# A two-block transformer step in fp32: selection in another order, a separate buffer at the seam between two product stages, and gate products among the stick-breaking items

## The reference, cut to what matters

```python
# PEER: 8 heads, 2 x 128 sub-keys, the top 16 of 16384 experts for each token and head
q = (t @ wq).reshape(128, 8, 2, 128)
s = einsum('tpcd,pckd->tpck', q, sub_keys)
s1, i1 = top_k(s[:, :, 0], 16);  s2, i2 = top_k(s[:, :, 1], 16)
top, pos = top_k(s1[..., :, None] + s2[..., None, :], 16)      # over 16 x 16 pairs
idx = i1 * 128 + i2 at pos;      g = softmax(top)
out = sum_k g_k * gelu(u[idx_k] . t) * v[idx_k]
...
# second block: projections of h, then
stick: z = q k / 8; w = sigmoid(z) * prod over later keys of sigmoid(-z), strictly causal; o_a = w v
soft:  an ordinary causal softmax over 64 + 32 (rotary) columns; q and k,v come from low-rank products
y_a = (o_a * silu(z_a)) @ w_branch_a;   y_b = (o_b * silu(z_b)) @ w_branch_b
x = x + gate * ((sigmoid(g_a) * y_a + sigmoid(g_b) * y_b) @ w_out);  out = rmsnorm(x)
```

## Time and profile before

| what | value |
|---|---|
| median of 3 runs | 2365.03 us (2364.62 to 2365.92) |
| the profiled execution's own time | 2369.11 us |
| its span, first to last instruction | 2367.3 us |
| mean granted TensorE clock in the span | 0.972 |

### The profile page before, as it was taken

How to read it: one execution, slowest core, us unless ns; L and a number is a source line. 1 busy time by engine, 2 the same in 40 slices (tenths; PEclk the granted TensorE clock), 3 DMA queues, 4 the chain that set the end, 5 groups by cost and what they waited for, 6 DMA issues and landing times. The chain is left out here.

```text
span 2367.3 us, 31784 instructions
## 1 busy us (share of the span) xinstructions
PE 2206.1 (93%) x12629; PEld 1966.4 (83%) x12629; DVE 1684.8 (71%) x2801; ACT 918.6 (39%) x1203; POOL 617.9 (26%) x354
## 2 busy tenths in 40 slices
PE   5999889988999998999999899999999896899997
PEld 2888777866799998999999899999999674576775
DVE  6555677873489999889876778788786656756543
ACT  4222234333233333566653233333333533576323
POOL 0000042322347667233333433333331000000000
PEclk8999999999999999999999999999999898899999
DMA  7567410012237777899999999999995222111222
GB/s 257 206 227 236 154 50 1 1 71 72 89 125 250 242 243 244 300 370 334 364 339 382 361 352 353 351 359 349 350 362 209 82 89 71 54 54 63 80 89 72
DMA packets 178100, 488.69 MB, mean 206 GB/s; under 512 B 13696, under 2 KB 80384, under 8 KB 166432
## 3 DMA queue, kind: packets, MB, share of 16 engines
q1 hardware_dynamic: 141088, 352.43, 43.6%
q0 software_dynamic: 36864, 134.23, 14.7%
HBM read 432.08 MB, written 52.43 MB: 205 GB/s over the span
## 5 line engine op out<-in xcount | busy, mean ns | idle before, releaser
L1087 PE MATMUL ps<-h_high,u_high 128*128 128x384 f32 (+1 forms) x1216 | 429.7, 353 | 21.7 <-POOL u_low L1305 11.9
L1089 PE MATMUL ps<-h_high,u_low 128*128 128x384 f32 (+1 forms) x1216 | 421.3, 346 | 0.0
L1088 PE MATMUL ps<-h_low,u_high 128*128 128x384 f32 (+1 forms) x1216 | 421.2, 346 | 0.0
L1087 PE MATMUL ps<-w_high,v_high 128*128 128x384 f32 x1024 | 343.6, 336 | 10.4 <-DVE w_low L1722 10.4
L1089 PE MATMUL ps<-w_high,v_low 128*128 128x384 f32 x1024 | 342.8, 335 | 0.0
L1088 PE MATMUL ps<-w_low,v_high 128*128 128x384 f32 x1024 | 342.8, 335 | 0.0
L1087 PEld LDWEIGHTS ps<-h_high,u_high 128*128 128x128 f32 x1216 | 231.5, 190 | 35.9 <-POOL u_low L1305 13.8
L1455 ACT ACTIVATE v_high<-v_raw 128x2048 fp32r<-128x2048 f32 x64 | 122.6, 1916 | 346.6 <-PE ps L1089 346.6
L1087 PE MATMUL ps<-h_high,w_high 128*128 128x512 f32 x560 | 226.7, 405 | 22.3 <-DVE w_low L346 7.5
L1089 PEld LDWEIGHTS ps<-h_high,u_low 128*128 128x128 f32 x1216 | 231.1, 190 | 8.1
L1088 PEld LDWEIGHTS ps<-h_low,u_high 128*128 128x128 f32 x1216 | 232.0, 191 | 7.1
(11 more groups left out here) (434 smaller groups left out, 4192.5 us busy)
## 6 DMA issues: line engine op xcount, KB each, us to landing
v_raw<-in_peer_v SPq DMA_DIRECT2D x64, 1024.0 KB
w_raw<-in_w SPq DMA_DIRECT2D x99, 512.0 KB, 3.5
u_first<-in_uT SPq DMA_DIRECT2D x32, 1024.0 KB
u_second<-in_uT SPq DMA_DIRECT2D x32, 1024.0 KB
xT<-in_late_w SPq DMA_DIRECT2D x56, 512.0 KB, 4.4
gelu_up<-gelu SPq DMA_DIRECT2D x128, 192.0 KB
gates<-gates_sb SPq DMA_DIRECT2D x12, 2048.0 KB, 12.6
weighted<-gelu_up SPq DMA_DIRECT2D x64, 384.0 KB
```

The source lines that it names most:

```text
L1087: pe.matmul(out, wh, mh, start=start, stop=False)
L1088: pe.matmul(out, wh, ml, start=False, stop=False)
L1089: return pe.matmul(out, wl, mh, start=False, stop=stop)
```

## The change

1. **Units.** They follow `UNIT_ORDER`: by head group over two token tiles (`SELF` and tile 0), then the other two tiles. The steps are 6, 7, 8, 9, 10, 12, 13, 15, 17, 20, 22, 24, 27, 29, 31, 34. The last unit of `SELF` is unit 5 at step 12 (`OWN_LAST`) where it was unit 3 at step 12.
2. **Picks.** 46 in steps 18 to 40, 66 in steps 41 to 68, 16 in steps 68 to 74. POOL issues the picks of a step after the low part of the next step.
3. **Batches** begin one tile later. `peer_v` rows begin at down step 1.
4. **The seam.** A buffer `gates_in` of its own takes the first gates, `gate_pair(0)` no longer waits for `u_raw`, `spill` runs one step earlier, and DVE and ACT prepare down step 1 before they turn to the dots and rows.
5. **Second block.** Two `uqm` tiles share a weight piece (4 pieces in place of 8). `ga` 0 and 1 and `sz` 0 to 2 (24 matmuls each) move to the first half, and slots are filled by the size of a product. `scores` of one item waits for its own bank alone, and DVE does `mask(n + 2)` right behind `finish(n)`.

```diff
-EARLY, MIDDLE = 40, 66
+FIRST_PICK, EARLY, MIDDLE = 18, 46, 66
+UNIT_ORDER = [(0, 0), (0, 1), (1, 0), (1, 1), (2, 0), (3, 0), (2, 1), (3, 1)] + [(c, t) for t in (2, 3) for c in range(4)]
+OWN_LAST = UNIT_ORDER.index((3, 0))
...
-    return OUT_G + 2 + 2 * u if u < 4 else OUT_G + 10 + 2 * (u - 4)
+    return OUT_G + (2, 3, 4, 5, 6, 8)[u] if u < 6 else OUT_G + 9 + 7 * (u - 6) // 3
...
-        return PICK_AT + (SPREAD_AT - PICK_AT) * n // EARLY
+        return FIRST_PICK + (SPREAD_AT - FIRST_PICK) * n // EARLY
...
-    return GROUPS - 7 + 7 * (n - EARLY - MIDDLE) // (PICKS - EARLY - MIDDLE)
+    return GROUPS - 8 + 7 * (n - EARLY - MIDDLE) // (PICKS - EARLY - MIDDLE)
...
-    return SPREAD_AT * EXPERT_TILES + m * SPREAD_G * EXPERT_TILES // BATCHES
+    return SPREAD_AT * EXPERT_TILES + 1 + m * (SPREAD_G * EXPERT_TILES - 1) // BATCHES
...
-    return n * (U_G - 3) // PICKS
+    return 1 + n * (U_G - 4) // PICKS
...
+        first_gates = sb("gates_in", [P, BLOCKS * 2 * GE * TB])
...
-                if g - 4 >= OUT_G + WQ_G:
-                    spill(g - 4)
+                if g - 3 >= OUT_G + WQ_G:
+                    spill(g - 3)
...
-            spill(GROUPS - 4)
+            gate_pair(0)
             load(0)
-
-            sp.wait_ge(u_split, OUT_PIECES + WQ_G + U_G - 1)
-            gate_pair(0)
             spill(GROUPS - 3)
             load(1)
             spill(GROUPS - 2)
-            sp.wait_ge(u_split, OUT_PIECES + WQ_G + U_G)
+            sp.wait_ge(u_split, OUT_PIECES + WQ_G + U_G - 1)
             gate_pair(1)
...
-                for n in picks_at[x + OUT_G]:
+                for n in picks_at[x + OUT_G - 1]:
...
+            high_v(1)
+            high_w(1)
             act.wait_ge(row_used, PICKS)
             act.activation(row_dot[:], row_dot[:], ACT.Gelu).then_inc(row_gelu, 1)
-            for g in range(1, U_G):
+            for g in range(2, U_G):
...
-            weigh(0)
-            low_v(0)
-            low_w(0)
+            for g in range(2):
+                weigh(g)
+                low_v(g)
+                low_w(g)
...
-    for h in range(NH):
-        piece("uq", h, [("uqm", h)])
-    for i in range(2):
-        piece("kn", i, [("kn", 4 * i + j) for j in range(4)])
+    for i in range(4):
+        piece("uq", i, [("uqm", 2 * i), ("uqm", 2 * i + 1)])
+    piece("kn", 0, [("kn", j) for j in range(4)])
+    piece("ga", 0, [("ga", 0)])
+    piece("sz", 0, [("sz", 0)])
+    piece("kn", 1, [("kn", 4 + j) for j in range(4)])
+    piece("ga", 1, [("ga", 1)])
     piece("kv", 0, [("kv", t) for t in range(4)])
-    for i in range(8):
+    for i in (1, 2):
+        piece("sz", i, [("sz", i)])
+    halfway = len(tiles)
+    for i in (2, 3):
         piece("ga", i, [("ga", i)])
...
                 for s in range(2):
+                    if p:
+                        pe.wait_ge(acted, 2 * p - 1 + s)
...
             def mask(n):
                 kind, h, i = items[n]
                 W = width(n)
-                dve.wait_ge(scored, 2 * (n // 2) + 2)
+                dve.wait_ge(scored, n + 1)
...
+            mask(0)
+            mask(1)
             for p in range(slots):
-                if p < PAIRS:
-                    mask(2 * p)
-                    mask(2 * p + 1)
                 for j in fill[p]:
                     if j in FIRST2:
                         low(TILES2[j][2] + 1)
                     evac(j)
+                for n in (2 * p, 2 * p + 1):
+                    if n < N:
+                        finish(n)
+                    if n + 2 < N:
+                        mask(n + 2)
                 if p >= 2 and (p - 2) % TT == TT - 1:
                     store((p - 2) // TT)
-                if p < PAIRS:
-                    finish(2 * p)
-                    finish(2 * p + 1)
```

More of the change, by code:

```diff
@@ L1257, in load @@
                 sp.dma_start(w[:, g % 2], gelu[g]).then_inc(w_in[g % 2], 16)
-            spill(GROUPS - 4)
+            written = 0
+            for g in range(GROUPS):
+                if g >= 2:
+                    sp.wait_ge(u_split, PIECES_BEFORE + g - 1)
+                if g:
+                    sp.dma_start(u_raw[g % 2][:], raw_of(g)).then_inc(u_in[g % 2], 16)
+                if g == 3:
+                    sp.dma_start(keys[:], k.dram["keysT"]).then_inc(keys_in, 16)
+                if g - 3 >= OUT_G + WQ_G:
+                    spill(g - 3)
+                while written < BLOCKS and g >= batch_place(PER_BLOCK * (written + 1) - 1) // GE + 4:
+                    sp.wait_ge(evac, 2 * PER_BLOCK * (written + 1))
+                    sp.dma_start(k.gates[:, written], gs[:, written % 2]).then_inc(wrote[written % 2], 16)
+                    written += 1
+            assert written == BLOCKS
+            for r in range(2):
+                sp.wait_ge(wrote[r], 16 * (BLOCKS // 2))
+            gate_pair(0)
             load(0)
-            sp.wait_ge(u_split, OUT_PIECES + WQ_G + U_G - 1)
-            gate_pair(0)
             spill(GROUPS - 3)
@@ L1299, in _ @@
             pool.tensor_tensor(u_low[:, 1], u_raw[1][:], u_high[:, 1].bitcast(F32), ALU.subtract).then_inc(u_split, 1)
-            for x in range(WQ_G + U_G):
+            for x in range(WQ_G + U_G + 1):
                 if x + OUT_G < SPREAD_AT:
@@ L1809, in second_tiles @@
     projected = len(tiles)
-    for h in range(NH):
-        piece("uq", h, [("uqm", h)])
-    for i in range(2):
-        piece("kn", i, [("kn", 4 * i + j) for j in range(4)])
+    for i in range(4):
[5 more added lines that the diff above has]
+    piece("ga", 1, [("ga", 1)])
     piece("kv", 0, [("kv", t) for t in range(4)])
-    for i in range(8):
+    for i in (1, 2):
+        piece("sz", i, [("sz", i)])
+    halfway = len(tiles)
+    for i in (2, 3):
         piece("ga", i, [("ga", i)])
+    piece("sz", 3, [("sz", 3)])
     for i in range(4):
-        piece("sz", i, [("sz", i)])
-    for i in range(4):
+        piece("ga", 4 + i, [("ga", 4 + i)])
         piece("bra", i, [("bra", 2 * i), ("bra", 2 * i + 1)])
@@ L1829, in second_tiles @@
         piece("wo", i, [("wo", i)])
-    return tiles, pieces, projected, attended
-TILES2, PIECES2, PROJECTED, ATTENDED = second_tiles()
+    return tiles, pieces, projected, halfway, attended
+TILES2, PIECES2, PROJECTED, HALFWAY, ATTENDED = second_tiles()
+PRODUCTS2 = {"uqm": 3, "kn": 2, "kv": 2, "ga": 8, "sz": 8, "bra": 4}
+EARLY_GA = 2
 BY_ACT = {"cq", "ckv", "sq", "sk", "uqm", "kn", "kv", "sz", "ga", "mz", "gb"}
@@ L1880, in piece_of @@
     elif name == "uq":
-        w = f["w_uq_2"][0][:, i * QKD:(i + 1) * QKD]
-        got = blocks(np.concatenate([w, swapped(w[:, NOPE:])], axis=1))
+        heads = [f["w_uq_2"][0][:, h * QKD:(h + 1) * QKD] for h in (2 * i, 2 * i + 1)]
+        got = np.concatenate([blocks(np.concatenate([w, swapped(w[:, NOPE:])], axis=1)) for w in heads], axis=1)
     elif name in ("kn", "kv"):
@@ L1964, in width, with first_gate @@
             return (items[n][2] + 1) * P
-        early, late = list(range(PROJECTED, tile_no("ga", 0))), list(range(tile_no("ga", 0), ATTENDED))
         slots = PAIRS + 2
+        soft_ready = tile_no("kv", 3) + 1
         fill = {p: [] for p in range(slots)}
-        for x, j in enumerate(early):
-            fill[x * HALF // len(early)].append(j)
-        for x, j in enumerate(late):
-            fill[HALF + x * (slots - HALF) // len(late)].append(j)
+        for first, end, slot, count in ((PROJECTED, HALFWAY, 0, HALF), (HALFWAY, ATTENDED, HALF, slots - HALF)):
+            sizes = [PRODUCTS2[TILES2[j][0]] for j in range(first, end)]
+            for x, j in enumerate(range(first, end)):
+                fill[slot + sum(sizes[:x]) * count // sum(sizes)].append(j)
+        def first_gate(n):
+            return mo[:, 2 + n, :] if n < EARLY_GA else merged[:, n, :]
         @block.sync
@@ L2036, in tile @@
                         pe.wait_ge(t_low, G0 + 5)
-                    w3, src = weights(j, 0, 3), [(ghi[:, t, :], glo[:, t, :]) for t in range(3)]
+                    w3, src = weights(j, 3 * (n % 2), 3), [(ghi[:, t, :], glo[:, t, :]) for t in range(3)]
                 elif kind == "kn":
@@ L2167, in evac @@
                 elif kind == "ga":
[L2168 removed]
+                    act.activation(first_gate(n), bank, ACT.Sigmoid).then_inc(act_read, 1)
                 elif kind == "gb":
```

37 lines of the change are left out of this document (10 added, 27 removed).

## The result

The changed kernel takes 2390.8 us (median of 4 runs, 2389.3 to 2393.7), the one before 2365.5 us (2364.6 to 2372.1): a ratio of 1.0092, 95% interval 1.0079 to 1.0106. It is 25 us slower where I forecast 32 us faster. The profiled execution has a span of 2387.5 us, 20.2 more than before.

A forecast was written before the change was run, and what follows sets the result against it. PE, busy 93% of the span, waits on POOL, held by DVE, in the selection; 15 + 3.5 + 11.5 + 2 = 32 us less, from 2365.0 to 2333 us, range 2324 to 2343, 2314 to 2352 with the faster rivals.

The forecast's parts named there:

- DVE's chain of selections: Sixteen selections and 46 dots on DVE up to the turn, without gaps from 602.1 us, ending at 924 us, 12 us sooner.
- the 64 for dots and the rest: In DVE's chain: 46 dots of 1.3 us (60) and 4 us of row numbers and softmax.
- the later ten selections: The last ten of the sixteen selections up to the turn, taken at 15.6 us each, 156 us in all.
- my slower rival: Port held in every selection: 18.5 us each, chain ends at 962 us, +6, 2371 us; decides from 18.1 us; chance 0.07.
- the 23.3 us that I gave as the most: Upper bound of one selection: 14.1 us plus two held products of 4.6 us each.
- laying five end to end over the low parts: Five early selections over POOL's low parts of steps 8 to 15: three to five products held, 17.5 us each taken.
- the ring of five: Row buffers for picks: span 2.5 steps where they spanned 3.1, so POOL may wait as much as before.
- The exponential: ACT's exponential of `SELF` at step 14 waits some 10 us, PE gets step 16 some 5 us late; not added.
- The wait of 3.6 us at the first batch: PE's wait for the first batch in the selection, claimed to go as a batch starts one tile later.
- The selection: Stretch up to the turn: DVE's chain ends sooner and the batch wait goes; 15 us booked, ends 0 and 23.
- Step 72 and the seam: PE's waits there shrink: 3.5 of 4.2 us booked at step 72, 11.5 of 12.4 at the seam.
- The slots: Attention slots: moved gate tiles grow the first half by 23 us and shorten the second by 25, -2 us.

The follow-up runs named there:

- e5: The changed kernel with POOL's low part of step g waiting for the dots of steps up to g - 2; ratio 1.0166 to the kernel before.
- e15: The changed kernel with units and picks' place as before, but 36 early picks, 72 in the spread stage and 20 late; ratio 1.0014 to the kernel before.
- e3: The changed kernel with only the picks as before (40 early from step 16, 22 late), units changed; ratio 0.9998 to the kernel before.
- e12: The changed kernel with ScalarE's exponential of the own tokens at step 16 in place of step 14; ratio 1.0078 to the kernel before.
- e1: The changed kernel with units, picks and first batch as before, seam and slots still changed; ratio 0.9945 to the kernel before.
- e4: The changed kernel with units and early picks as before (40 from step 16), 16 late picks, seam and slots still changed; ratio 0.9913 to the kernel before.
- e2: The changed kernel with only the units' order and steps as before, picks still changed; ratio 1.0131 to the kernel before.
- e6: The changed kernel with four row buffers in place of five; ratio 1.0037 to the kernel before.
- e9: The changed kernel with GpSimd's low part as two instructions of half the columns each; ratio 1.0063 to the kernel before.

## Why the prediction was wrong

*The step that failed* is DVE's chain of selections: "I take 14.1 us for the first, 17.5 for units 1 to 5 and 15.6 for the later ten: 14.1 + 87.5 + 156 + 64 = 322, so 924 us". Measured, from 601.0 us: 14.1 + 90.6 + 169.4 + 102.0 = 376.1, so 977.1 us. Of the 54 us that I was short, 38 are in the 64 for dots and the rest. I costed every dot at 1.3 us, near the median of 1.22, with the 5.67 us of the earlier trace rows in view: eight held dots are 35 us, two waits for late rows 11 and the held product of the row numbers (L1673) 4; only 42 dots were done by then, at 1.15 us each, which takes 12 off. 13 are in the later ten selections, whose two products I took as seldom held (16.9 us each in the end), and 3 in units 1 to 5.

The mechanism, POOL's low part holding a DVE product, was on my list, and so was the sign: my slower rival had it at 18.5 us in every selection. Selections took 17.1 us in the mean, under the 18.1 from which that rival decides, so it has the sign by another term than its own. I had counted two products of a selection that can be held, L1622 and L1644. There are more: L1629, L1650 and L1653 of the changed kernel were held once each, 13 us in all, so the 23.3 us that I gave as the most rests on too short a list (the longest selection took 22.1). And I left out the other kind altogether, the dot. The sentence "laying five end to end over the low parts" did what was needed for units 1 to 5, and came out; for the rest I took a mean, where the two engines run in step and one meeting is repeated in each unit. "the ring of five spans 2.5 steps where it spanned 3.1, so POOL may wait as much as before" stopped short of asking what POOL does right after that wait.

By the Trainium skill ("SBUF — State Buffer", section "SBUF: two separate sides") the pair of ports goes to whichever starts first, for the whole instruction. The traces agree for the dot at 796.02 us, which starts 0.24 us behind the low part and ends 1.1 us after it, and the other way round in e5, where the third dot starts 0.2 us ahead and the low part takes 5.35 us in place of 4.6. They don't agree for L1624 in e15 (at 824.28 us), which starts 0.4 us ahead of the low part and is held all the same, in four units, and in e3 twice. My use of the rule was the slip: I applied it to a selection's products only, though a dot has two inputs there as well.

*Point by point.* Selections without idle time from 602 us: right. The exponential waits some 10 us: 12.5; that it isn't added: right, by e12. The wait of 3.6 us at the first batch goes: wrong, 1.2 us at 993 and 2.8 at 1001 us stand in its place. The selection: -15 forecast, +41.6 measured. Step 72 and the seam: -15 forecast, -14.2 measured, no wait of PE over 1 us there, and none at down step 2. That the two numbers are so near is partly luck: it is 17.0 gained there (5.3 and 11.7 where I booked 3.5 and 11.5), less 2.8 lost between the turn and step 66, where I had nothing. By e1 against e4 the seam's part needs the fewer late picks; the gates' buffer and the order alone leave 8.7 us of waits. The slots: 128.2 us (I said 130) and 109.6 (112), together -7.2 where I said -2; the mechanism was right, both halves 2 us better than booked.

*The best of both.* e4 keeps seam, late picks and slots, and has units and early picks as before: 0.9913, 20 us faster than the kernel before and some 42 faster than the changed one.

*Still open:* how much of the 12.5 us of e3 against e1 is the packing's own holds and how much the stall at the exponential, and whether some spacing of requests keeps 46 early dots free of holds; and why L1624 is held although it starts first.

## What to carry to other kernels

Where two engines can block each other for the length of an instruction, and one restarts the other once per period, don't take a mean of the collisions: lay one period of both over each other, instruction by instruction, with the number of items that the change puts between. A collision then came in period after period or not at all (nine periods in a row in e2), and one request more or fewer moved it. And cost every kind of instruction that can be held, not only the ones that were held before.

## What was not expected of the hardware

- A fourth dot held for 4.3 us costs more than the three in front of it together, and a kernel with a smaller ring of buffers (e6) or more dots (e4 against e15: 0.9913 and 1.0014) can be the faster one.
- In e9 two GpSimd instructions of 2.4 us back to back held a VectorE product of 128x64 over both (4.26 us), while a dot got in between the two and made the pair last 5.81 us in place of 4.72.
- The last product of the softmax takes 0.56 us, and 4.03 in the kernel before: that was a hold as well (3.5 us that the 28.6 don't count), which I had read as its price.
